# The dense feed-forward part: gate-up product computed transposed, down product in PSUM banks 0 to 3

## The reference

```python
D_FF = ((8 * D_MODEL // 3 + 255) // 256) * 256          # 2816
...
        hn = (_rms(x, norm2_g[l]) * (1 + sc2) + sh2).astype(x.dtype)
        gate, up = jnp.split(hn @ w_gate_up[l], 2, axis=-1)
        x = x + g2 * ((jax.nn.silu(gate) * up) @ w_down[l])
```

## Time and profile before

| | |
|---|---|
| time, median of 3 runs | 1569.79 us (1567.9 to 1571.73) |
| span of the profiled execution, first to last instruction | 1568.5 us |
| PE busy | 1475.2 us, 94% of the span |
| DVE busy | 324.1 us, 21% |
| ACT busy | 221.4 us, 14% |
| HBM read | 495.44 MB |
| dense part, from its first gate-up matmul to the last instruction | 1327.9 to 1568.5 us |

### The profile page before, as it was taken

One profiled execution on the slowest core, in us unless ns is written; L12 is line 12 of the kernel. 1 busy time (PEld: TensorE's weight loads), 2 busy tenths in 40 slices (PEclk: granted clock), 3 DMA queues, 4 the chain that ended last, 5 costly groups with the idle time before them and its releaser, 6 DMA issues.

```text
span 1568.5 us, 18813 instructions
## 1 busy us (share of the span) xinstructions
PE 1475.2 (94%) x7278; PEld 787.3 (50%) x7278; DVE 324.1 (21%) x861; ACT 221.4 (14%) x405; POOL 21.8 (1%) x14
## 2 busy tenths in 40 slices
PE   7999999999999999999999999999699998999998
PEld 5655443343343343343333334334499664888843
DVE  5535321121111121121111111112312533000001
ACT  1321011011111011011011111101212430000100
POOL 3100000000000000000000000000000000000000
PEclk9998999999999999999999999999799968999999
DMA  9996999999999999999999999999944103444400
GB/s 331 351 407 264 357 419 417 416 419 419 415 418 419 416 418 418 418 417 418 419 416 419 418 416 418 419 417 414 295 156 156 54 1 107 135 152 143 134 0 27
DMA packets 127123, 496.98 MB, mean 317 GB/s; under 512 B 9825, under 2 KB 51506, under 8 KB 91026
## 3 DMA queue, kind: packets, MB, share of 16 engines
q1 hardware_dynamic: 126484, 495.47, 79.9%
q10 hardware_dynamic: 606, 1.06, 0.2%
HBM read 495.44 MB, written 1.05 MB: 317 GB/s over the span
## 4 chain that ended last, share of the span: by engine, by line
PE 59%; DMA 20%; SPq 15%; DVE 3%; issue 2%; ACT 1%; DVEq 0%; ACTq 0%
DMA ring<-in_w_gate_up_dram 19%; PE PS L989 10%; SPq L459 9%; PE PS L803 9%; PE PS L545 8%; PE PS L828 8%; SPq L462 5%; PE PS L789 5%; PE PS L1005 5%; PE PS L695 3%; PE PS L836 3%; PE PS L644 2%; PE PS L528 1%; ACT work L1155 1%; PE PS L670 1%
## 5 line engine op out<-in xcount | busy, mean ns | idle before, releaser
L803 PE MATMUL PS<-ring,work 128*64 128x512 f32 x2048 | 461.4, 597 | 25.5 <-DMA ring<-in_w_gate_up_dram 25.5
L803 PEld LDWEIGHTS PS<-ring,work 128*64 128x64 f32 x2048 | 138.0, 137 | 331.1 <-issue 232.2
L828 PE MATMUL PS<-ring,work 128*64 128x512 f32 x1024 | 225.1, 592 | 0.0
L1624 DVE TENSOR_SCALAR work<-PS 128x512 f32<-128x512 f32 x32 | 22.1, 691 | 679.9 <-PE PS L803 679.9
L989 PE MATMUL PS<-ring,cols 128*128 128x256 f32 x704 | 156.0, 383 | 2.1 <-issue 2.1
L989 PEld LDWEIGHTS PS<-ring,cols 128*128 128x128 f32 x704 | 134.7, 192 | 20.8 <-DVE cols L1331 2.5
L828 PEld LDWEIGHTS PS<-ring,work 128*64 128x64 f32 x1024 | 71.7, 137 | 132.0 <-issue 129.6
L545 PE MATMUL PS<-ring,cols 128*128 128x240 f32 (+3 forms) x576 | 121.8, 374 | 4.1 <-DVE cols L1331 2.1
L789 PE MATMUL PS<-work,rows 128*128 128x64 f32 x1056 | 125.0, 278 | 0.0
L789 PEld LDWEIGHTS PS<-work,rows 128*128 128x128 f32 x1056 | 123.8, 196 | 0.8 <-DVE work L1601 0.8
L545 PEld LDWEIGHTS PS<-ring,cols 128*128 128x128 f32 x576 | 110.4, 196 | 13.4 <-DVE cols L1331 2.5
(11 more groups left out here) (261 smaller groups left out, 859.6 us busy)
## 6 DMA issues: line engine op xcount, KB each, us to landing
ring<-in_w_gate_up_dram SPq DMA_DIRECT2D x278, 1024.0 KB, 20.4
ring<-in_w_down_dram SPq DMA_DIRECT2D x139, 1024.0 KB, 22.2
ring<-in_w_ada_dram SPq DMA_DIRECT2D x24, 1024.0 KB, 15.9
ring<-in_w_in_dram SPq DMA_DIRECT2D x13, 960.0 KB, 10.8
ring<-in_w_out_dram SPq DMA_DIRECT2D x8, 1024.0 KB, 10.9
ring<-in_w_in_dram SPq DMA_DIRECT2D x3, 1024.0 KB, 12.8
x_sb<-in_x_dram SPq DMA_DIRECT2D x2, 512.0 KB, 3.8
work<-in_band_dram SPq DMA_DIRECT2D x1, 1024.0 KB, 14.9
```

What stands on the lines that cost most here:

```text
L803: mm = pe.matmul(bank(b)[CAP * h:CAP * (h + 1), :], xg[:, k, :], w[:, b * FE + h * 512:b * FE + (h + 1) * 512], start=False, stop=(k == KD ...
L828: mm = pe.matmul(bank(3)[CAP * h:CAP * (h + 1), :], lhs, w[:, (f % 2) * D + h * 512:(f % 2) * D + (h + 1) * 512], start=False, stop=(f == 7))
```

## The change

In the gate-up product the two operands change places: 128 columns of the weight chunk are stationary now, and `cols[:, k, :]`, all 256 tokens, is moving. The loop over the 2 token tiles becomes a loop over the 2 tiles f of 128 hidden columns of a chunk. The number of matmuls, their sizes and their banks stay. The product has hidden columns on the partitions, which is the form that the down product needs. So DVE's product goes straight into `h_t`, and the transposes on PE, ACT's copies, `h_rows`, and the semaphores `h_turned` and `h_cols` are gone. The down product waits for `h_ready` of pair 9 at its start and of pair 10 ahead of its last two chunks, and accumulates in banks 0 to 3, from which `add_gated` reads.

```diff
-            for j in range(PAIRS + 1):
-                if j < PAIRS:
-                    if j >= 2:
-                        pe.wait_ge(sig["h_ready"], j - 1)
-                    if j == 1:
-                        pe.wait_ge(sig["bcast_kept"], 2)
-                    for up in range(2):
-                        n = N_GU2 + 2 * j + up
-                        need(n)
-                        for t in range(NT):
-                            for k in range(KD):
-                                mm = pe.matmul(bank(4 + 2 * (j % 2) + up)[:, t * CW:(t + 1) * CW],
-                                               cols[:, k, t * P:(t + 1) * P], chunk(n)[:, k, :],
-                                               start=(k == 0), stop=(k == KD - 1))
-                        mm.then_inc(chunk_used, 1)
-                if j >= 1:
-                    i = j - 1
-                    pe.wait_ge(sig["h_ready"], i + 1)
-                    if i >= 2:
-                        pe.wait_ge(sig["h_cols"], i - 1)
+            for j in range(PAIRS):
+                if j >= 2:
+                    pe.wait_ge(sig["h_ready"], j - 1)
+                if j == 1:
+                    pe.wait_ge(sig["bcast_kept"], 2)
+                for up in range(2):
+                    n = N_GU2 + 2 * j + up
+                    need(n)
                     for f in range(2):
-                        for t in range(NT):
-                            mm = pe.transpose(bank(i % 2)[:, f * T + t * P:][:, 0:P],
-                                              h_rows[:, i % 2, t * CW + f * P:t * CW + (f + 1) * P], ident)
-                    mm.then_inc(sig["h_turned"], 1)
+                        for k in range(KD):
+                            mm = pe.matmul(bank(4 + 2 * (j % 2) + up)[:, f * T:(f + 1) * T],
+                                           chunk(n)[:, k, f * P:(f + 1) * P], cols[:, k, :],
+                                           start=(k == 0), stop=(k == KD - 1))
+                    mm.then_inc(chunk_used, 1)
...
-                    mm = pe.matmul(bank(4 + 2 * t + h), h_t[:, f, t * P:(t + 1) * P],
+                    mm = pe.matmul(bank(2 * t + h), h_t[:, f, t * P:(t + 1) * P],
...
-            pe.wait_ge(sig["h_cols"], PAIRS)
+            pe.wait_ge(sig["h_ready"], PAIRS - 1)
...
             need(N_END - 1)
+            pe.wait_ge(sig["h_ready"], PAIRS)
...
-            for j in range(PAIRS + 1):
-                if j < PAIRS:
-                    act.wait_ge(chunk_used, N_GU2 + 2 * j + 1)
-                    if j >= 2:
-                        act.wait_ge(sig["h_ready"], j - 1)
-                    do.tell(nc.scalar.activation(h_sil[:, j % 2, :], bank(4 + 2 * (j % 2)), ACT.Silu), "silu_ready")
-                if j >= 1:
-                    i = j - 1
-                    act.wait_ge(sig["h_turned"], i + 1)
-                    do.tell(nc.scalar.copy(h_t[:, 2 * i:2 * i + 2, :],
-                                           bank(i % 2).rearrange("p (f t) -> p f t", f=2)), "h_cols")
+            for j in range(PAIRS):
+                act.wait_ge(chunk_used, N_GU2 + 2 * j + 1)
+                if j >= 2:
+                    act.wait_ge(sig["h_ready"], j - 1)
+                do.tell(nc.scalar.activation(h_sil[:, j % 2, :], bank(4 + 2 * (j % 2)), ACT.Silu), "silu_ready")
...
-                if j >= 2:
-                    dve.wait_ge(sig["h_turned"], j - 1)
-                do.tell(v.tensor_tensor(h_rows[:, j % 2, :], h_sil[:, j % 2, :], bank(5 + 2 * (j % 2)), ALU.mult),
+                do.tell(v.tensor_tensor(h_t[:, 2 * j:2 * j + 2, :],
+                                        h_sil[:, j % 2, :].rearrange("p (f t) -> p f t", f=2),
+                                        bank(5 + 2 * (j % 2)).rearrange("p (f t) -> p f t", f=2), ALU.mult),
                         "h_ready")
             dve.wait_ge(sig["bcast_kept"], 2)
-            dve.wait_ge(sig["h_turned"], PAIRS)
             for t in range(NT):
-                add_gated(4, t, "out_ready", 2, N_END)
+                add_gated(0, t, "out_ready", 2, N_END)
```

More of the change, by code:

```diff
@@ L164 @@
 conv_sum conv_tanh conv_silu qk_sq sq_used heads_ready heads_turned heads_cols ml_exp ml_m ml_guard ml_tanh
-bcast_done bcast_kept gate_used silu_ready h_ready h_turned h_cols out_ready out_stored""".split()
+bcast_done bcast_kept gate_used silu_ready h_ready out_ready out_stored""".split()
 class Steps:
@@ L306, in two_blocks @@
         h_sil = work[:, FT * T:FT * T + 1024].rearrange("p (b n) -> p b n", b=2)
-        h_rows = rows[:, :, 0:512]
         def slot(n):
```

## The result

| | before | after |
|---|---|---|
| median | 1568.82 us (8 runs, 1564.78 to 1571.73) | 1559.12 us (8 runs, 1557.27 to 1565.27) |
| ratio, 95% interval | | 0.9948 (0.9936 to 0.9960) |
| span of the profiled execution | 1568.5 us | 1555.5 us |
| from the first gate-up matmul to the end of the span | 240.6 us | 234.7 us |

The kernel became faster, by 8.2 us as the ratio has it (6.3 to 10.0), where 6.4 us were forecast. The median of after lies 1.9 us under the low end of the range. The two profiled spans differ by 13.0 us, and the dense part holds 5.9 of them. The other 7.1 us stand ahead of it, where the two programs are the same. Much of what follows is about these 7 us.

What follows compares the result with a forecast made beforehand. PE's instructions, one after another, were taken to bound the dense part; 3.9 us for transposes and 2.5 us for the hand-over, 6.4 us in all, came off 1569.8 us, giving 1563.4 us, range 1561.0 to 1566.8.

Steps and rivals of the forecast that it cites:

- What bounds the kernel: Dense part: PE's instructions one after another, busy 99.8 of 99.8 us, so time leaving PE's row leaves the run.
- Point 1, transposes: Gate-up: nine groups of four PE transposes between pairs go, at 0.44 us each by starting times, 3.9 us saved.
- Point 2, hand-over: Before the down product: last two transpose groups and waits for DVE's product and ACT's copy go, 2.5 us saved.
- Points 3 to 6: Exchanged gate-up operands, DVE's product into `h_t`, SP's chunk loads, down product in banks 0 to 3: no cost or gain.
- slow weight loads: Gate-up: loading 128 columns from `ring` exceeds the 216 ns step, making the kernel slower, up to 1587 us; chance 0.04.
- the exposed first load: Gate-up: each of 22 chunks' first weight load is no longer hidden, costing 4.2 us, so 1567.6 us; chance 0.07.
- the full durations: Gate-up: removed transposes give back 273 ns each, 9.8 us in place of 3.9, so 1557.5 us; chance 0.02.
- The sum: Dense part: 3.9 us for transposes plus 2.5 us for the hand-over, 6.4 us, giving 1563.4 us, 0.41% less.
- How the numbers follow: Whole run: chances of faster 0.87, same 0.09, slower 0.04, and the range 1561.0 to 1566.8 us around 1563.4.
- the clock's part: Start of gate-up: the low clock's 2.6 us loss should stay the same, but could move the sum about 2 us either way.
- theory S: Ahead of the dense part: the changed program is also faster there, by 2 us or more; stated with the experiments.

Runs made afterwards that it cites:

- With eight in a group: Kernel after with nine groups of eight transposes, read by nobody, put back on PE between pairs: 1569.89 us, ratio 1.0007 to the kernel before.
- with fillers: Kernels plus 29 unread bf16 matmuls ahead of the dense part and 52 ahead of the second block's projection: before 1562.29 us, after 1556.58 us.

## Why the prediction was right in its sum and wrong in its range

**What bounds the kernel** held: PE's row in the dense part, with no other engine near it.

**Point 1, transposes, 3.9 us:** right, 3.97 measured with fillers. Reading the price from starting times and not from the row's 273 ns was the step that mattered. With eight in a group a group costs 0.87 us, twice the 0.44, and nine groups 7.9.

**Point 2, hand-over, 2.5 us:** right, 2.54. Nothing was late next; the first down matmul stood ready behind the last gate-up matmul.

**Points 3 to 6, all at zero:** right. The kernel with the operands as they were has the same two rows, number for number. The down product took 75.55 us in place of 75.81. For the operands, zero was right for a milder reason than the one given: the prediction says that the stationary operand "has just come in", and the trace has it in the ring about 70 us ahead of its use. The rivals of slow weight loads (0.04), of the exposed first load (0.07) and of the full durations (0.02) are all excluded by runs for this kernel.

**The sum, 6.4 us:** right. 6.55 us in the dense parts with fillers, 5.9 in the first two profiles (6.5 without the clock's loss), and in the ratios 8.2 (6.3 to 10.0) and 6.6 (4.2 to 8.9).

**How the numbers follow: the step that failed.** The mechanism and the 6.4 us held; what failed is the time they were taken from and the range around it. The range ran from 1561.0 to 1566.8, and the median was 1559.12. The forecast was 4.3 us too high, in three pieces. The base was the median of three runs, 1569.79; with eight runs it is 1568.82, 1.0 us less, and in three later comparisons the same kernel had 1567.76, 1567.03 and 1565.44. The ratio holds 1.8 us more than the sum; its interval (6.3 to 10.0) just holds the 6.4, so this can be scatter. The rest, 1.5 us, is the place of two medians in their samples: the means of the eight and eight runs are 1568.57 and 1560.37, 8.2 us apart like the ratio, and the median of before lies 0.25 over its mean, that of after 1.25 under it. So a part of the miss is the draw: the second sample of the same kernel had 1560.98, at the edge of the range. But a range that such a draw leaves was too narrow. The prediction made it from "the spread of the runs and the clock, each about 2 us", the spread being that of three runs, and put the clock's part in the dense part alone: "What stands before it is unchanged, so I expect the same loss." What stands before was unchanged, but the loss was not the same (2.35 us and 2.97 in the first two profiles, 1.38 in the next), and the stages ahead had losses of their own. The profiles show three places that scatter by themselves: 149.3 to 155.1 us for the start of the expert loop, 39.12 to 42.13 for the start of the projection, 1.6 us between two profiles of the same kernel for the start of gate-up. The sign was in the chain of the kernel before, and I didn't weigh it, since the change doesn't touch that stage:

```profile
1125.18 42.13 PE PS L545 x192
1167.30 0.44 PE PS L909 x4
1167.74 6.48 PE PS L545 x32
```

32 MATMULs in 6.48 us would make 38.9 for 192, and 39.12 were measured at full clock; the stage had lost 3.0 us. A range for a time has to hold the scatter of all stages, though the sum needs only those that the change touches.

I also carried over 1.3 us between the span and the median. In the runs that list both, the time is 1.8 to 1.9 us over its own span (1557.27 and 1555.5 in the first of after). By that the profiled execution of before took about 1570.3 us, an estimate, 1.5 above the median of its eight, while the profiled one of after, 1557.27, was the fastest of its eight, 1.85 under their median. These two distances, 3.3 us, are why the spans differ by 13.0 us and the medians by 9.7. The forecast of the time isn't touched by it, since it takes the 6.4 from the median.

**Open:** whether anything of theory S exists. Without fillers the two ratios average a little over 7 us, with fillers the medians have 5.7, the traces 6.55. Nothing in them needs a further cause, and nothing excludes 1 us of one. By their ratios before and after are 5.0 us apart with fillers. What moves the start of the expert loop between 149 and 155 us wasn't tried.

## What to carry to other kernels

If the result of a product is transposed only to be contracted again, exchange stationary and moving operand in the first product: with the same sizes, and weights that lay ready long before, it cost nothing here, and the transposes, copies and the wait at the hand-over go. Price the small instructions in a full engine row by the distance of starting times with and without them, not by their durations. When a change is worth 0.4% and the stages around it scatter as much, compare the stage in the traces, and take the range of the total from the scatter of every stage.

## What the runs showed of the hardware that I had not expected

Ahead of the dense part PE waits for 1.74, 3.27 and 2.12 us, with 8 transposes after each of the first two waits. The granted clock was 1.00 in the stretch of the first wait (1318 to 1321 us), fell in that of the second (0.74) and stayed at 0.50 through the third and the first 4 us of gate-up. The hand-over left it at 1.00, but it was no idle gap of 2.3 us, as the prediction has it: PE was busy for 1.08 of it, and waited for 0.51 and 0.73 us. Matmuls whose result nobody reads, put into such gaps, kept it at 1.00 and gave back 1.4 to 3.0 us of a stage of 152 us; 81 of them in two places, without the change, made the kernel before faster by themselves (0.9971, 0.9957 to 0.9986), and with the change the ratios were 0.9915 and 0.9939, where the change alone had 0.9948 and 0.9958.
